# Issuing the next expert's weight loads before waiting for the current expert's to land

## The reference

```python
def _grouped_experts(x2, idx, wts, w_eg, w_eu, w_ed):
    ...   # assignments sorted by expert, each expert's segment padded to blocks of 128 rows
    def run(a):
        xblk, e = a
        return _swiglu(xblk, w_eg[e], w_eu[e], w_ed[e])
    yb = lax.map(run, (xb, block_e)).reshape(n_rows, Dm)
    ...
    y = (yb[dest_flat].reshape(T, K, Dm).astype(jnp.float32) * wts[..., None]).sum(axis=1)

def _swiglu(x, wg, wu, wd):
    return (jax.nn.silu(x @ wg) * (x @ wu)) @ wd
```

```
expert  0-15: 1 1 1 1 1 1 2 1 2 1 1 1 2 1 1 1      expert 16-31: 1 1 1 1 2 1 1 2 1 1 1 1 1 1 1 1
expert 32-47: 3 2 1 2 2 1 2 3 1 1 2 1 2 2 1 2      expert 48-63: 1 1 1 1 1 1 1 1 1 1 1 1 2 2 1 1
```

## Time and profile before

| | us |
|---|---|
| Three runs | 2263.2, 2283.53, 2288.75; median 2283.53 |
| The profiled execution: its own time | 2278.31 |
| Its span, first to last instruction | 2276.5 |
| Busy: TensorE, VectorE, ScalarE, GpSimd | 2005.9, 889.3, 509.0, 396.4 |
| First matmul of the routed experts' first block starts at | 1143.59 |
| The last block's `gate_up` starts at | 2193.86 |

### The profile page before, as it was taken

How to read it: one execution, slowest core, us unless ns; L and a number is a source line. 1 busy time by engine, 2 the same in 40 slices (tenths; PEclk the granted TensorE clock), 3 DMA queues, 4 the chain that set the end, 5 groups by cost and what they waited for, 6 DMA issues and landing times.

```text
span 2276.5 us, 28877 instructions
## 1 busy us (share of the span) xinstructions
PE 2005.9 (88%) x8246; PEld 1052.2 (46%) x8247; DVE 889.3 (39%) x2410; ACT 509.0 (22%) x933; POOL 396.4 (17%) x345
## 2 busy tenths in 40 slices
PE   4797899998887989889889999998999999998980
PEld 1456555444552435464344544454455545543450
DVE  2826500135873222235323333333333333332338
ACT  3422210005771110232111111111111111111122
POOL 0010000004552030000011221212122222211214
PEclk7898889998998899988989999999999999999995
DMA  9641200010104520021278998998988797898853
GB/s 337 244 157 24 117 0 0 1 74 9 39 2 136 180 102 0 29 92 52 100 283 271 298 301 286 305 287 281 298 259 251 205 300 248 270 298 268 274 122 126
DMA packets 100878, 394.20 MB, mean 173 GB/s; under 512 B 27279, under 2 KB 30003, under 8 KB 71996
## 3 DMA queue, kind: packets, MB, share of 16 engines
q1 hardware_dynamic: 70020, 302.44, 35.8%
q0 software_dynamic: 24768, 90.19, 16.6%
q10 hardware_dynamic: 6024, 0.73, 0.3%
HBM read 329.16 MB, written 62.57 MB: 172 GB/s over the span
## 4 chain that ended last, share of the span: by engine, by line
PE 29%; DMA 23%; issue 6%; SPq 4%; DVE 3%; ACT 1%; POOL 0%; POOLq 0%; DVEq 0%; ACTq 0%
DMA arena<-in_w_exp_down 23%; PE psum L992 11%; PE psum L1020 6%; PE psum L862 5%; SPq L2277 2%; PE psum L978 1%; SPq L2273 1%; SPq L2272 1%; DVE arena L1642 1%; PE psum L889 1%; PE psum L841 1%; PE psum L895 1%; DVE arena L1652 1%; PE psum L902 0%; PE psum L885 0%
## 5 line engine op out<-in xcount | busy, mean ns | idle before, releaser
L992 PE MATMUL psum<-arena 128*128 x1360 | 626.8, 615 | 48.8 <-SPq L2298 42.7
L992 PEld LDWEIGHTS psum<-arena 128*128 128x128 f32 x1360 | 259.3, 196 | 349.1 <-issue 349.1
L1020 PE MATMUL psum<-arena,tail 128*128 x672 | 302.3, 592 | 0.0
L2125 POOL DMA_INDIRECT moe_rows<-arena x84 | 133.4, 1588 | 803.6 <-ACT arena L1976 264.8
L1598 DVE TENSOR_TENSOR arena<-arena,psum 128x256 f32<-128x256 f32 x85 | 35.8, 421 | 488.2 <-ACT arena L1962 488.2
L1020 PEld LDWEIGHTS psum<-arena,tail 128*128 128x128 f32 x672 | 121.1, 190 | 120.5 <-issue 120.5
L1962 ACT ACTIVATE arena<-psum 128x256 f32<-128x256 f32 x85 | 32.6, 384 | 633.0 <-PE psum L992 633.0
L689 PE MATMUL psum<-arena 128*128 128x512 f32 (+1 forms) x384 | 126.7, 493 | 0.0
L862 PE MATMUL psum<-arena 128*128 128x512 f32 (+1 forms) x288 | 124.4, 593 | 0.3 <-ACT arena L1879 0.3
L1576 DVE TENSOR_TENSOR arena<-tail,arena 128x1152 bf16<-128x1152 f32 x89 | 119.6, 1344 | 0.0
L1976 ACT ACTIVATE arena<-psum,arena 128x512 f32<-128x512 f32 x84 | 57.7, 687 | 213.4 <-PE psum L1020 208.2
(11 more groups left out here) (492 smaller groups left out, 2378.0 us busy)
## 6 DMA issues: line engine op xcount, KB each, us to landing
arena<-in_w_exp_gate SPq DMA_DIRECT2D x64, 1024.0 KB, 5.3
arena<-in_w_exp_up SPq DMA_DIRECT2D x64, 1024.0 KB, 9.1
arena<-in_w_exp_down SPq DMA_DIRECT2D x64, 1024.0 KB, 12.2
arena<-in_w_ada SPq DMA_DIRECT2D x24, 1024.0 KB, 7.8
arena<-in_w_ada_final SPq DMA_DIRECT2D x8, 1024.0 KB, 6.5
arena<-in_cache_k SPq DMA_DIRECT2D x32, 256.0 KB, 3.4
arena<-in_cache_v SPq DMA_DIRECT2D x32, 256.0 KB, 2.9
arena<-in_w_in SPq DMA_DIRECT2D x1, 6176.0 KB, 18.5
```

The costliest lines, as they stand in the source:

```text
L992: ins = pe.matmul(slot[2 + par].rearrange("p (h n) -> p h n", h=2), xTs[:, par, k, :], ring_gu[:, at, :, k, :].rearrange("p a h n -> p (a ...
L1020: ins = pe.matmul(slot[1][:, n * 512:(n + 1) * 512], hTs[:, k, :], ring_d[:, at, k, n, :].rearrange("p a n -> p (a n)"), start=(k == 0), s ...
L2125: pool.indirect_dma_start(y_dram, bass.IndirectOffsetOnAxis(ap=s_idx[:, par:par + 1], axis=0), y_buf[:, par, :], None, compute_op=ALU.add) ...
```

## The change

SyncE issues the load of expert n+1 first, and then waits for the landing of expert n and announces it. The wait inside `load_expert` for the slot's release stays where it was in that function, so it, too, now stands ahead of the announcement of n. The semaphore counts are adapted to the shift. No other engine's instructions change.

```diff
             sp.sem_inc(shared_stored, 1)
-            sp.wait_ge(ld_ring[0], 48)
-            sp.sem_inc(weights_in, 1)
-
-            with sp.Fori(0, E // RING - 1) as j:
+
+            with sp.Fori(0, (E - 1) // RING) as j:
                 for i in range(RING):
-                    q = (i + 1) % RING
-                    load_expert(j * RING + (i + 1), q)
-                    sp.wait_ge(ld_ring[q], (j + 1) * 48 if q else (j + 2) * 48)
+                    load_expert(j * RING + (i + 1), (i + 1) % RING)
+                    sp.wait_ge(ld_ring[i], (j + 1) * 48)
                     sp.sem_inc(weights_in, 1)
-            for q in range(1, RING):
-                load_expert(E - RING + q, q)
-                sp.wait_ge(ld_ring[q], 48 * (E // RING))
+            for n in range((E - 1) // RING * RING, E):
+                if n + 1 < E:
+                    load_expert(n + 1, (n + 1) % RING)
+                sp.wait_ge(ld_ring[n % RING], 48 * (n // RING + 1))
                 sp.sem_inc(weights_in, 1)
             sp.wait_ge(routed_done, 1)
```

## The result

| | us |
|---|---|
| Before, median of 6 runs | 2283.32 (2263.2 to 2292.22) |
| With the change, median of 6 runs | 2220.66 (2216.59 to 2226.32) |
| Ratio, 95% interval | 0.9738 (0.9703 to 0.9772) |
| Profiled execution with the change: own time, span | 2221.51, 2219.7 |

The change saves 62.7 us between the medians and 56.8 between the two profiled executions. The forecast was 2223. The runs also lie closer together here, 10 us from lowest to highest against 29; but 15 later runs of the kernel before spanned only 12 us, so no cause for that is shown.

What follows compares the result with a forecast made beforehand. TensorE, 88% busy, was taken to lose 66.8 us in the routed stage, mostly to loads chained one at a time. Last gate_up 60.6 us sooner, less 5 us residue, is 55.6 off 2278.3: 2223 us, range 2207 to 2248.

Steps and rivals of the forecast that it cites:

- The start: First gate_up of the routed stage: expert 1's loads are issued before expert 0's announcement, so it starts 3.9 us later.
- The hole: DMA moves 22 GB/s for 3.3 us around each next issue; loading ahead closes it, making a one-block expert's cycle 12.9 us.
- What stalls remain: Runs of one-block experts: each uses up 1.2 us of a 10 us lead, leaving a residue of 5 us.
- The sum: Last gate_up 60.6 us sooner, less 5 us of residue: 55.6 us saved, 2223 us against the profiled 2278.3.
- SyncE's waits: Sign in SyncE's queue: waits on the third load stay in number, shorter in runs; slot waits grow well above 71.0 us.
- the term of nothing: Outside runs of one-block experts the ring is full and loads wait for slots, so nothing changes; costed at nothing.
- The announcement behind the release wait: SyncE's announcement of n also waits for the slot of n+1; costed at nothing under 10.7 us of cover.
- GpSimd's transfers: Queued weights slow GpSimd's scatter by their presence, not their number; its 12.66 us fits in the 12.9 us already charged.
- Rival B: More queued loads slow GpSimd's scatters, landing after 15 to 18 us; gain only 35.5 us, 2243 us; chance 0.12.
- D: GpSimd's scatter loop becomes the bound, 13.2 us for all 84 blocks; slower, 2341 us; chance 0.04.
- Rival C: DMA engines can't carry more over a whole cycle, which stays 15 us; only the late start remains, 2282 us; chance 0.06.

Runs made afterwards that it cites:

- The version that announces first: The changed kernel, but expert 0 is announced before expert 1's loads are issued, as before the change; 2219.34 us, ratio 0.9718.
- the halved kernel: The changed kernel with the second half of gate_up's contraction left out; 2161.77 us in one run, against 2243.51 for the kernel before with the same cut.
- the version with the shorter hole: The kernel before, with SyncE reading the next expert's two table values ahead of the landing wait, loads still issued after it; 2241.9 us, ratio 0.9816.
- the last version: The changed kernel with expert 1's loads and expert 0's announcement moved ahead of the wait for the shared expert's stores; 2215.77 us, ratio 0.9704.

## Why the prediction was right

*The start* was priced at 3.9 us. The first gate_up came 16.0 us after expert 0's load before and 19.2 after: 3.2. The version that announces first takes it back.

*The hole.* Shown. Closing part of it gave 42 us between the medians, closing it all the rest, and the traffic of a run of one-block experts rose to 338 GB/s.

*What stalls remain: the step that was mis-sized.* The residue was put at 5 us, since a one-block expert was to cost the DMA engines 12.9 us (bounds 12.0 and 13.3) and so use up 1.2 us of the lead each time. It was 0. The lead itself was right, 10.6 us against 10; but it is still 10.2 us eight one-block experts later, so such an expert cost at most 11.7 us, less than the lower bound. Both ways of pricing came from the kernel before: 350 GB/s are from 11 us inside one load, and the time per MB is a mean over the whole kernel. With the queues full for 94 us, 359 GB/s moved.

*The sum.* 55.6 us predicted, 56.8 between the profiled executions, by terms that cancel: 5.0 more from the missing residue, 0.7 from the start, 0.5 behind the last block, 0.1 less for a longer first step, and 4.9 less, because expert 0's load was issued at 1132.50 instead of 1127.57. That the two large ones cancel is luck. The last term is not the change's: already the last matmul of an early stage (L555), far ahead of the edit, starts at 178.3 us instead of 170.5, and in the other kernels here at 175.4 to 177.9. So the profiled execution of before was a quick one at its start, as it lay 5 us under the median; the medians' 62.7 us are nearer to what the routed stage gave, 64.4 less 3.2. Why the first 170 us vary was not looked into.

*SyncE's waits.* Those for a slot grew as foretold, to 711.2 us. Those for a landing were to stay in number and get shorter; they fell from 63 to 14, because SyncE now waits for the next slot first and mostly finds the load landed when it comes to look. The ground given for "nothing changes" outside the runs was also too strong: in the stretch 1632 to 1990 of the kernel before, SyncE waited 10 times for a slot and 20 times for a landing, so the ring was not simply full there. TensorE waited for neither, before or after, and so the term of nothing held.

*The announcement behind the release wait*, costed at nothing under 10.7 us of cover. Right, and the cover is real: take one expert's worth of it away, by order or by a slot, and 67 us of the routed stage are lost.

*GpSimd's transfers.* The median landing of a scatter rose from 8.7 to 10.5 us and GpSimd now waits 233.6 us for its own scatters in 27 waits, but TensorE waits for a gathered row only once, 4.8 us ahead of its first block. I had taken that presence and not depth counts, and the halved kernel bears it out. Rival B is out, and so is D: its 13.2 us per block would have had to be seen in the changed kernel, whose blocks are 11.708 us apart, and even where TensorE is off the bound and loads are nearly always queued GpSimd's loop takes 12.13. That is little slack, though: with a faster TensorE this loop is what one meets next. What the Trainium skill says of queues taken in turn (DMA: Bandwidth & Descriptors, "Queues, rings and completion order") agrees with the halved kernel's trace, where a load took up to 19.1 us and no scatter more than 12.3. The Trainium skill's 425 GB/s for a transfer of 16 MB (the same page, "Measured") is for transfers issued from GpSimd. It was not reached by full queues here: 335 to 359 over the stretches shown, so the measurement decides.

*Rival C* (hole not the limit) fell with the first result.

## What to carry to other kernels

A loop that issues a load, waits for it and issues the next left the DMA engines nearly idle around each issue here (22 GB/s for 3.3 us of some 15), even with free slots in the ring; compare the wait for landings with the wait for slots to see it. Issue one ahead, but look at what the issue itself waits for: an announcement that stands behind a slot's release needs as many blocks of cover as that release takes, and one step further it cost a little more than the change had brought. Ask how many cheap items in a row use up the lead, and trust a price per item only as far as it comes from a stretch with full queues: where the old kernel has none, as here, the price can be too high.

## What was not expected of the hardware

In the runs of one-block experts of the kernel before, waits of 0.7 to 2.2 us ahead of a gate_up left it at 7.13 us, while those of 3.2 us and more were followed by gate_ups of 8.8 to 10.1 us. A stall made shorter can thus be worth more than its length. Between the two it was not regular. In the version with the shorter hole, waits of 2.26 and 2.41 us left the gate_up at 7.13 us, one of 2.65 was followed by 8.82, and so was a shorter one:

```profile
1581.42 8.83 PE L992 MATMUL psum<-arena 128*128 x16 [1.99 <-SPq L2277]
```

At the start, too, the second gate_up, behind a wait of 2.4 us, took 7.13 us in the changed kernel and 8.82 in the last version. The length of the wait alone doesn't tell which it will be.
